# Latent attention in a two-block kernel: raw exponentials transposed, row sums by a matrix of ones, scaling on each head's output

## The reference, cut to what matters

```
def one_block(args):
    q_blk, blk = args
    s = jnp.einsum('bqhd,bkhd->bhqk', q_blk, k, preferred_element_type=jnp.float32) * scale
    q_idx = blk * Q_BLOCK + jnp.arange(Q_BLOCK)
    s = jnp.where(k_idx[None, :] <= q_idx[:, None], s, -jnp.inf)
    p = jax.nn.softmax(s, axis=-1)
    return jnp.einsum('bhqk,bkhd->bqhd', p.astype(v.dtype), v, preferred_element_type=jnp.float32)
...
o = causal_block_attention(q, k, v)            # 8 heads of 128
y = jax.nn.sigmoid(gate_a) * y_a + jax.nn.sigmoid(gate_b) * y_b      # y_b is o, flattened
x = x + g_m * (y @ w_out)
```

## Time and profile before

| what | value |
|---|---|
| median of 3 runs | 3191.84 us |
| lowest and highest of them | 3183.66 and 3198.17 us |
| the profiled execution's own time | 3186.11 us |
| its span | 3184.3 us |
| instructions in it | 28078 |
| mean granted TensorE clock | 0.899 |
| busy: TensorE, VectorE, ScalarE | 88%, 56%, 30% of the span |

### The profile page before, as it was taken

How to read it: one execution, slowest core, us unless ns; L and a number is a source line. 1 busy time by engine, 2 the same in 40 slices (tenths; PEclk the granted TensorE clock), 3 DMA queues, 4 the chain that set the end, 5 groups by cost and what they waited for, 6 DMA issues and landing times. The chain is left out here.

```text
span 3184.3 us, 28078 instructions
## 1 busy us (share of the span) xinstructions
PE 2792.2 (88%) x11102; PEld 2020.6 (63%) x11102; DVE 1767.7 (56%) x2478; ACT 958.6 (30%) x1236; POOL 0.2 (0%) x4
## 2 busy tenths in 40 slices
PE   6997749999999499999977679999999677799998
PEld 2783313478888278887743337888877433478886
DVE  2645441486665875667783338565587733463333
ACT  1322311143232241333542224222335422232222
POOL 0000000000000000000000000000000000000000
PEclk8997868999999799999986669999999766799999
DMA  5111121134543135443210003454332100022322
GB/s 213 53 67 40 59 84 53 73 123 164 180 164 143 66 144 182 163 166 111 93 48 17 22 1 125 146 199 162 136 110 89 43 9 22 27 90 87 108 85 81
DMA packets 57083, 313.99 MB, mean 99 GB/s; under 512 B 5911, under 2 KB 9367, under 8 KB 36088
## 3 DMA queue, kind: packets, MB, share of 16 engines
q1 hardware_dynamic: 56952, 312.19, 27.2%
HBM read 310.07 MB, written 2.10 MB: 98 GB/s over the span
## 5 line engine op out<-in xcount | busy, mean ns | idle before, releaser
L430 PE MATMUL psum<-x_hi,w_hi 128*128 128x512 f32 x1968 | 784.6, 399 | 10.8 <-DVE squares L1150 10.8
L431 PE MATMUL psum<-x_lo,w_hi 128*128 128x512 f32 x1968 | 768.6, 391 | 0.0
L432 PE MATMUL psum<-x_hi,w_lo 128*128 128x512 f32 x1968 | 768.4, 390 | 0.0
L1201 DVE TENSOR_TENSOR w_lo<-w_raw,w_hi 128x2048 fp32r<-128x2048 f32 (+1 forms) x192 | 418.5, 2181 | 295.0 <-ACT w_hi L819 293.2
L819 ACT ACTIVATE w_hi<-w_raw 128x2048 fp32r<-128x2048 f32 (+1 forms) x192 | 350.6, 1827 | 538.0 <-DMA w_raw<-in_w 537.3
L430 PEld LDWEIGHTS psum<-x_hi,w_hi 128*128 128x128 f32 x1968 | 371.0, 188 | 105.0 <-issue 20.0
L432 PEld LDWEIGHTS psum<-x_hi,w_lo 128*128 128x128 f32 x1968 | 370.6, 188 | 78.5
L431 PEld LDWEIGHTS psum<-x_lo,w_hi 128*128 128x128 f32 x1968 | 371.1, 189 | 77.8 <-issue 4.8
L430 PE MATMUL psum<-hidden_hi,w_hi 128*128 128x512 f32 x912 | 358.6, 393 | 0.0
L431 PE MATMUL psum<-hidden_lo,w_hi 128*128 128x512 f32 x912 | 355.1, 389 | 0.0
L432 PE MATMUL psum<-hidden_hi,w_lo 128*128 128x512 f32 x912 | 354.9, 389 | 0.0
(11 more groups left out here) (330 smaller groups left out, 2946.4 us busy)
## 6 DMA issues: line engine op xcount, KB each, us to landing
w_raw<-in_w SPq DMA_DIRECT2D x160, 1024.0 KB, 4.9
ada_w<-in_ada SPq DMA_DIRECT2D x96, 768.0 KB, 6.3
w_raw<-in_w SPq DMA_DIRECT2D x32, 704.0 KB, 4.0
w_raw<-in_ada SPq DMA_DIRECT2D x20, 768.0 KB, 5.0
big<-in_ada SPq DMA_DIRECT2D x12, 768.0 KB, 11.9
big<-in_w_uq SPq DMA_DIRECT2D x8, 384.0 KB, 3.1
residual<-in_xT SPq DMA_DIRECT2D x1, 2048.0 KB, 15.2
small<-in_lru_w SPq DMA_DIRECT2D x2, 1024.0 KB, 6.9
```

The source lines that it names most:

```text
L430: mm(o, w_h, x_h, start=first, stop=False)
L431: mm(o, w_h, x_l, start=False, stop=False)
L432: return mm(o, w_l, x_h, start=False, stop=last)
L1201: v.tensor_tensor(wl[:, r, 0:n], raw[:, r, 0:n], wh[:, r, 0:n].bitcast(f32), ALU.subtract).then_inc(w_split.sem, 1)
```

## The change

The exponentials are no longer scaled before they are transposed, so W is gone and T(n) waits for E(n) itself. E no longer accumulates. The sums of the rows come from TensorE: beside each of the four matmuls of V stands one of the same width with `ones` as the stationary operand, into bank 0 (even head) or 1 (odd head), which leaves each query's sum on all 128 partitions. H begins with the reciprocal of that 128x512 bank, multiplies the values by it (this multiplication now raises `head2`), and goes on with gate, sum and split. Since banks 0 and 1 are also P's, P waits until both heads of the pair before have raised `head2`, and the output projection waits for all eight.

```diff
@@ TensorE
                     if pair == 0:
                         eng.wait_ge(evacuated.sem, hybrid[l][4].evac0)
+                    eng.wait_ge(S("head2").sem, HEADS2 * l + 2 * pair)
                     for o in range(9):
...
                         if n + 1 < n0 + 8:
                             scores2(n + 1)
-                        eng.wait_ge(S("weights2").sem, S("weights2").next(me))
+                        eng.wait_ge(S("exp2").sem, n + 1)
                         eng.wait_ge(S("turned2").sem, max(0, n))
...
                                 ins = mm(ps[:, 7, j * P:T], V2[:, j, hd * P:(hd + 1) * P], extra[:, j, j * P:T],
                                          start=j == 0, stop=j == 3)
-                            me.count(ins.then_inc(S("values2").sem, 1), S("values2"))
+                                total = mm(ps[:, hd, j * P:T], ones[:], extra[:, j, j * P:T], start=j == 0, stop=j == 3)
+                            me.count(total.then_inc(S("values2").sem, 1), S("values2"))
+                eng.wait_ge(S("head2").sem, HEADS2 * (l + 1))
                 products(hybrid[l][4], xh, xl)
@@ ScalarE
                         me.count(act(big[:, 30 + n % 2, 0:keys], B(4 + n % 2, keys), ACT.Exp,
-                                             bias=negmax[:, n % 2:n % 2 + 1], scale=192 ** -0.5,
-                                             accum_out=sums[:, n % 2:n % 2 + 1]).then_inc(S("exp2").sem, 1), S("exp2"))
+                                             bias=negmax[:, n % 2:n % 2 + 1], scale=192 ** -0.5).then_inc(S("exp2").sem, 1), S("exp2"))
@@ VectorE
                             max2(n + 1)
-                        eng.wait_ge(S("exp2").sem, S("exp2").next(me))
-                        me.count(v.reciprocal(rsum[:, c:c + 1], sums[:, c:c + 1]).then_inc(me.done.sem, 1), me.done)
-                        eng.wait_ge(*me.own())
-                        e = big[:, 30 + n % 2, 0:(q + 1) * P]
-                        me.count(v.tensor_scalar(e, e, rsum[:, c:c + 1], None, ALU.mult).then_inc(S("weights2").sem, 1), S("weights2"))
-                        eng.wait_ge(*me.own())
                         if q == 3:
                             eng.wait_ge(S("values2").sem, S("values2").next(me))
-                            me.count(v.tensor_tensor(t1[:], B(7), big[:, 8 + hd, :], ALU.mult).then_inc(S("head2").sem, 1), S("head2"))
+                            me.count(v.reciprocal(t1[:], B(hd % 2)).then_inc(me.done.sem, 1), me.done)
+                            eng.wait_ge(*me.own())
+                            me.count(v.tensor_tensor(t1[:], B(7), t1[:], ALU.mult).then_inc(S("head2").sem, 1), S("head2"))
+                            eng.wait_ge(*me.own())
+                            me.count(v.tensor_tensor(t1[:], t1[:], big[:, 8 + hd, :], ALU.mult).then_inc(me.done.sem, 1), me.done)
                             eng.wait_ge(*me.own())
                             me.count(v.tensor_tensor(t1[:], t1[:], big[:, hd, :], ALU.add).then_inc(me.done.sem, 1), me.done)
```

## The result

| what | before | after |
|---|---|---|
| median | 3192.49 us (6 runs) | 3218.24 us (6 runs) |
| ratio, 95% interval | | 1.008 [1.0063, 1.0096] |
| the profiled execution's own time | 3186.11 us | 3220.41 us |
| its span | 3184.3 us | 3218.6 us |
| the two attention stages | 237.24 + 233.05 us | 245.98 + 247.54 us |

The changed kernel is slower by 0.8%, 26 us. One of its six executions took 11410 us at a mean granted clock of 0.228; the ratio leaves it out, and the median of the other five is 3217.72 us. The runs with a profile differ by 34.3 us of span, of which 7.3 are no matter of the change: its first attention stage begins at 1672.67 instead of 1665.42 us, behind a part that is the same in both. In the twelve kernels of this study that start lies between 1665.4 and 1675.9. So what follows compares stages by their lengths.

What follows compares the result with a forecast made beforehand. The prediction took a ring of waits to bound the attention stages, not TensorE's work. Six pairs at +3.4 us and two at -0.5 gave +19 us, 3205 beside the profiled execution, 3208 as forecast, range 3176 to 3226.

Steps and rivals of the forecast that it cites:

- the forecast's case: Attention stages: TensorE's clock falls early between S0 and V3, making a pair 3.4 us longer; chance 0.50.
- 1, S0 to V3: First half of a pair: T(n) needs only E(n) and C(n-1), so 20.2 us become 14.6, gain 5.6.
- 2, V3: First head's V: doubled matmuls, partly at 1.2 GHz, take 7.0 us, 2.6 more.
- 3, V3's end to T5: Between the heads: W4 is gone but M5 waits behind a longer H3; gain 0.65 us of 9.65.
- 4, T5 to V7: Second head's last steps: 9.89 us become 8.8, gain 1.1.
- 5 and 6, V7 and the wait: End of a pair: doubled V7 costs 2.6 us more, and TensorE idles 4.45 us before P.
- 7, P: Start of the next pair: P runs at a fallen clock after the idle time, 11.0 us, 1.1 more.
- The walk: Attention pair: the new order stepped through with old durations, putting V3's start 14.6 us after S0, or 10.7 with clock up.
- with the clock up until T3 and down for V3: First pair of each layer: S0 to V3 gains 9.5 us, so the pair's sum is -0.5 us.
- pays this instead: Behind a layer's last pair: the output projection, not P, bears the 1.1 us of fallen clock.
- the 0.65 that I named: Attention stage: mean TensorE clock about 0.65 expected as a sign, against over 0.75 if the clock stayed up.
- Rival A: Attention pairs: clock stays up from P to V3's end, -3.1 us a pair, -25 us, 3164 us; chance 0.13.

Runs made afterwards that it cites:

- hold: The changed kernel with one more wait on TensorE: T(n) also waits until M(n+1) is done; 3268.85 us, ratio 1.0249.
- before_totals: The kernel before, with the four matmuls by ones added beside those of V into bank 3, never read; 3219.44 us, ratio 1.0089.
- bank3_m5: bank3 with M5 put directly behind H3's reciprocal on VectorE; 3113.29 us, ratio 0.9754.
- bank3_wait: bank3 with both waits for H put back, ahead of P and of the output projection; 3200.12 us, ratio 1.0025.
- bank3: The changed kernel with the sums in bank 3, P's outputs in banks 0 to 2 and both waits on `head2` gone; 3142.38 us, ratio 0.9847.
- no_recip: The changed kernel with VectorE's 128x512 reciprocal replaced by a copy, so values are multiplied by the sums; 3133.18 us, ratio 0.9814.
- before_swapped: The kernel before, with W(n) moved ahead of M(n+1) on VectorE; 3106.26 us, ratio 0.9729.
- one_total: The changed kernel with one 512-column matmul by ones per head replacing the four, leaving the sums out; 3180.6 us, ratio 0.9965.

## Why the prediction was right, and where it was not

The forecast was 3208 us in a range of 3176 to 3226; 3218.24 came, 10 above it. Of those 10 us, 3.5 are the kernel before, whose median came out at 3192.49 and not at 3189; the other 6.7 are the change's, 25.8 us for 19. The six pairs that follow another pair went by the forecast's case almost term by term (mean of six, after less before):

| item | predicted | measured |
|---|---|---|
| 1, S0 to V3 | -5.6 (14.6 long) | -5.9 (14.3 long) |
| 2, V3 | +2.6 | +2.7 |
| 3, V3's end to T5 | -0.65 | -0.3 |
| 4, T5 to V7 | -1.1 | -0.9 |
| 5 and 6, V7 and the wait | +7.05 | +6.6 |
| 7, P | +1.1 | +1.45 |
| sum | +3.4 | +3.6 |

- **Items 1 and 4** took their size from the overlap. hold shows it to be the larger part of item 1, 27.1 of 47.1 us, and only 2.2 of item 4's 7.5. (The rest of hold's 50.6 us is M5 behind H3.) The prediction's sentence that W's instructions "are worth nothing beside it" does not stand: item 1's other 20.0 us are about the time that W took between M(n+1) and T(n), 2.3 us a pair. The walk had its total right because it left W out as well.
- **Item 2** is confirmed by itself: 2.3 us a V in before_totals. In the changed kernel V3 and V7 run cold for 3.5 to 5.4 us and at 2.4 GHz after.
- **Item 3** was small for the reason given: W4 is gone, but H3 grew by 4.1 us in front of M5. bank3_m5 takes 26.9 us out of it. The difference to -0.65 lies in the kernel before, where one pair took 8.08 us and one 9.01 instead of the 9.65 that I read in a single pair.
- **Items 6 and 7** had the right size: 4.29 us for 4.45, and P to S0 11.2 for 11.0. The 11.0 was a value chosen between two ends, though, not a walk. And the items price one consequence of the wait, P's own length; between bank3_wait and bank3 the wait also costs 5.8 us in S0 to V3 and 5.1 in V3 to S5.
- **The step that failed** is "with the clock up until T3 and down for V3 ... I expect this in the first pair of each layer". There, S0 to V3 took 15.86 us in both layers, 5.9 and 5.6 less than before instead of 9.5. The clock rose 3.7 and 5.3 us into P, later than in other pairs (3.1 to 3.5), but fell right ahead of T0 all the same, 13.9 and 15.5 us in. Shorter V's than forecast (6.3 and 6.7 us for 7.0) and a shorter V7 and wait (together +6.1 and +6.3 for +7.05) paid part of that back, by luck: the two pairs came to -0.2 and +1.6 us, not to -0.5 each, and the six others to +21.7, not +20.4.
- **The output projection** behind each layer's last pair "pays this instead", said the prediction; its sum holds 1.1 us for each of the two. It starts cold, and its first eight products take 1.6 us longer in layer 0 and 1.3 in layer 1. The parts behind the stages grew by 3.1 and 0.7 us; why these differ is open.
- Together the stages gave 23.2 us for the 19 of the sum; with those 3.8 it is 27.0, and the medians differ by 25.8. The mean clock in the stage, 0.70, was above the 0.65 that I named. The prediction shows no working for that figure; in the trace the clock stays up for 6.8 us from the second half of each V on, where it stayed up for 3.4 us behind V3 in seven of the eight pairs before.

**Rival A** was the near miss. It got 0.13 and did not come, but in bank3_wait, with the same work and the same waits, five pairs of eight follow its walk in S0 to V3 (11.14 us to V3 where it said 10.7). Its second condition, a V3 at 2.4 GHz, was met in none of the kernels for the whole of V3: the clock falls around V3's start, 21.4 us into P in bank3, and V3 to S5 stays at 6.1. By the Trainium skill (TensorE: Matmul & The Clock Gate, "HAM oscillation — how this bites in real kernels") gaps between bursts throttle TensorE and closing them keeps it fast. As a rule of direction this holds in bank3, no_recip and before_swapped, where more was gained than the gaps were long (in before_swapped TensorE's idle time in the stages fell by 55 us, from 136.4 to 81.4, and the stages by 86.7). As a rule for one place it did not do: in the changed kernel the clock fell at T0 behind 9.44 us of work in 10.20, and in one_total it stayed up to V3 although the gap of 4.29 us ahead of P was still there.

**Where the expected gain of such a change goes.** 47 us of S0 to V3 were really there, and the doubled V's (38), the wait before P (34) and its cold P (8) ate them and the 10 of items 3 and 4. bank3 gives back the wait and the cold P, and before_swapped shows that a gain of this size in S0 to V3 (54.6 us) was to be had without the change.

## What to carry to other kernels

Ahead of rewriting the arithmetic to take a small instruction out of a ring of waits, look at what stands in front of it on its engine: swapping W(n) with M(n+1) brought 85 us, while the change that removed W, with all that it put in W's place, cost 26. When a result moves to a buffer that the next stage also uses, price the wait for its slowest reader (here a 3.36 us reciprocal of a broadcast sum) and the cold clock behind it: between bank3_wait and bank3, 36 us of waits made 58. Put long work that nobody waits for (H3) behind the short steps that the ring waits for.

## What the runs showed of the hardware that was not expected

- A gap before P costs more than its length. With 4.29 us of idle TensorE the clock reads 0.50 at P's start; without it (bank3) the clock stays at 1.00 from the middle of V7 to V3's start, 24 us on end, and the stages are 54.7 us shorter than in bank3_wait, for 36.1 of waits. Whether S2 falls back to 1.2 GHz later does not follow from the gap: with the same 4.29 us it does in the changed kernel, and does not in five pairs of bank3_wait and six of one_total.
- Two executions with 9.44 and 9.50 us of TensorE's work in 10.20 us went different ways for the next 6.6 us, one at 1.2 GHz and one at 2.4. Windows of busy time don't predict the clock at this point.
- VectorE's reciprocal takes 3.36 us on 128x512 numbers and 0.16 on 128x1, where a product takes 0.69 on 128x512. A sum that is spread over all partitions before it is inverted pays the first price: 53.7 us in 16 heads where the 64 small ones cost 10.5.
